# Expert stage of a two-block transformer kernel: the first expert bias added by VectorE instead of TensorE, spread over the partitions by GpSimd

## The reference, cut to what matters

```python
hcat = x_pad[tok] @ w1[e] + b1[e]                 # 128 x 1024 times 1024 x 2048
x_glu = jnp.minimum(hcat[:, ::2], 7.0)
x_lin = jnp.clip(hcat[:, 1::2], -7.0, 7.0)
act = x_glu * jax.nn.sigmoid(1.702 * x_glu) * (x_lin + 1.0)
y = act @ w2[e] + b2[e]                           # 128 x 1024 times 1024 x 1024
```

## Time and profile before

| | us |
|---|---|
| median of 3 runs | 3118.15 |
| lowest and highest | 3116.43, 3118.99 |
| the profiled execution | 3108.3 |
| its span, first to last instruction | 3106.5 |
| TensorE busy in the span | 2924.3 (94%) |
| VectorE busy | 2114.3 (68%) |
| ScalarE busy | 1586.4 (51%) |
| GpSimd busy | 280.5 (9%) |

### The profile page before, as it was taken

One profiled execution on the slowest core, in us unless ns is written; L12 is line 12 of the kernel. 1 busy time (PEld: TensorE's weight loads), 2 busy tenths in 40 slices (PEclk: granted clock), 3 DMA queues, 4 the chain that ended last, 5 costly groups with the idle time before them and its releaser, 6 DMA issues. The chain is left out here.

```text
span 3106.5 us, 46231 instructions
## 1 busy us (share of the span) xinstructions
PE 2924.3 (94%) x18534; PEld 2342.4 (75%) x18534; DVE 2114.3 (68%) x2176; ACT 1586.4 (51%) x1765; POOL 280.5 (9%) x225
## 2 busy tenths in 40 slices
PE   5999999789999999999999959899899999899999
PEld 4777777468887888887888847688778877678877
DVE  6578644569999999989999975466464454366642
ACT  3556433347777777777777734222354542333321
POOL 0110100001111111111111000344000000000000
PEclk9999999789999999999999979899899998999999
DMA  6332343269999999999999972000221222323321
GB/s 247 128 106 89 110 134 109 109 253 367 374 375 363 372 378 375 373 369 371 373 371 369 370 277 68 16 4 4 92 67 59 75 70 81 109 82 94 95 82 68
DMA packets 217372, 607.95 MB, mean 196 GB/s; under 512 B 10784, under 2 KB 118304, under 8 KB 183424
## 3 DMA queue, kind: packets, MB, share of 16 engines
q1 hardware_dynamic: 202480, 554.87, 48.3%
q0 software_dynamic: 14592, 50.36, 4.7%
q10 hardware_dynamic: 144, 0.53, 0.0%
HBM read 582.62 MB, written 23.10 MB: 195 GB/s over the span
## 5 line engine op out<-in xcount | busy, mean ns | idle before, releaser
L2491 DVE TENSOR_TENSOR weight_ring_part<-weight_ring,weight_ring_part 128x2048 fp32r<-128x2048 f32 x380 | 852.9, 2286 | 104.3 <-ACT weight_ring_part L2430 103.5
L2430 ACT ACTIVATE weight_ring_part<-weight_ring 128x2048 fp32r<-128x2048 f32 x380 | 713.7, 1915 | 255.7 <-PE ps L193 137.5
L193 PE MATMUL ps<-weight_ring_part 128*128 128x512 f32 x1456 | 576.8, 396 | 0.0
L189 PE MATMUL ps<-weight_ring_part,gathered_hi 128*128 128x512 f32 x1024 | 408.6, 399 | 0.0
L293 DVE TENSOR_TENSOR weight_ring_part<-weight_ring,weight_ring_part 128x2048 fp32r<-128x2048 f32 x111 | 253.2, 2281 | 225.5 <-ACT weight_ring_part L290 223.6
L193 PE MATMUL ps<-weight_ring_part,gathered_hi 128*128 128x512 f32 x1024 | 405.2, 396 | 0.0
L192 PE MATMUL ps<-weight_ring_part,gathered_lo 128*128 128x512 f32 x1024 | 405.1, 396 | 0.0
L189 PE MATMUL ps<-h1T_hi,weight_ring_part 128*128 128x512 f32 x872 | 357.5, 410 | 3.1 <-DVE weight_ring_part L293 1.7
L192 PE MATMUL ps<-h1T_hi,weight_ring_part 128*128 128x512 f32 x872 | 346.0, 397 | 0.0
L193 PEld LDWEIGHTS ps<-weight_ring_part 128*128 128x128 f32 x1456 | 275.3, 189 | 68.9
L290 ACT ACTIVATE weight_ring_part<-weight_ring 128x2048 fp32r<-128x2048 f32 x111 | 211.1, 1902 | 135.8 <-PE ps L193 104.0
(11 more groups left out here) (491 smaller groups left out, 4382.9 us busy)
## 6 DMA issues: line engine op xcount, KB each, us to landing
weight_ring<-in_w SPq DMA_DIRECT2D x190, 2048.0 KB, 8.8
weight_ring<-in_w_in SPq DMA_DIRECT2D x58, 1024.0 KB, 5.2
weight_ring<-in_w_ffn_up SPq DMA_DIRECT2D x44, 512.0 KB, 4.9
weight_ring<-in_w_ffn_down SPq DMA_DIRECT2D x11, 1024.0 KB, 4.8
mod_tile<-in_w_ada POOLq DMA_DIRECT2D x36, 256.0 KB, 3.1
weight_ring<-in_w_ada SPq DMA_DIRECT2D x8, 1024.0 KB, 12.9
gate_rows<-in_w_ada POOLq DMA_DIRECT2D x28, 256.0 KB, 3.1
weight_ring<-in_w_branch SPq DMA_DIRECT2D x6, 1024.0 KB, 5.2
```

Of the source, the lines that this page charges most:

```text
L189: first = nc.tensor.matmul(out, x[0], y[0], start=start, stop=False)
L193: return nc.tensor.matmul(out, x[0], y[1], start=False, stop=stop)
L2430: nc.scalar.activation(hi_half(h), full_half(h), ACT.Copy).then_inc(w_rounded, 1)
L2491: nc.vector.tensor_tensor(lo_half(h), full_half(h), hi_half(h), ALU.subtract).then_inc(w_split, 1)
```

## The change

b1 is loaded as two rows of 1024 numbers, into partition 0 of a tile that is free by then and of a new one. GpSimd spreads each to all 128 partitions (`spread_bias`, two partition broadcasts of 1024 elements). TensorE's four bias matmuls go, and so do the rounding and the split of b1; the first product now opens the PSUM bank. VectorE adds the bias while it reads PSUM: first both pieces of `glu`, then both of `lin`, then, after a drain, one clamp of the whole `lin` (128 x 1024). `glu` is clamped by GpSimd (`clamp`, two pieces of 512), and ScalarE's activation waits for that. On GpSimd's queue the clamp of expert e+1 stands ahead of the scatter of e, and the spread of e+2 behind it. SyncE loads the next b1 once the last one is spread. The scatter gets a bound, so that slots without a token are skipped.

```diff
-        b1_pick = sb(experts, "b1_pick", [36, 4], F32R)
-        b1_full = sb(experts, "b1_full", [4, 512])
-        b1_parts = sb(experts, "b1_parts", [36, 512], F32R)
+        b1_late = sb(experts, "b1_late", [1, DFF])
+        b1_rows = (gate_rows[0:1, 0, :], b1_late[:, :])
+        b1_wide = sb(experts, "b1_wide", [P, 2 * DFF])
...
-                    sp.dma_start(b1_full[:, :], row.rearrange("e (n f) -> (e n) f", n=4)).then_inc(b1_loaded, 16)
+                    for n in range(2):
+                        sp.dma_start(b1_rows[n], row[:, DFF * n:DFF * n + DFF]).then_inc(b1_loaded, 16)
...
                     if t.more:
-                        sp.wait_ge(used, t.half(0)[0] + (1 + free0))
+                        sp.wait_ge(b1_ready, t.i + 1)
                         load_b1(t.e + 1)
...
+                def spread_bias(r, e):
+                    pool.wait_ge(b1_loaded, 32 * (r * E + e) + 32)
+                    if e:
+                        pool.wait_ge(bias_added, r * E + e)
+                    for n in range(2):
+                        last = nc.gpsimd.partition_broadcast(b1_wide[:, DFF * n:DFF * n + DFF], b1_rows[n], channels=P)
+                    last.then_inc(b1_ready, 1)
+
+                def clamp(r, e):
+                    for s in range(2):
+                        half = slice(512 * s, 512 * s + 512)
+                        pool.wait_ge(glu_ready, (r * E + e) * 2 + (s + 1))
+                        nc.gpsimd.tensor_scalar(glu[:, half], glu[:, half], LIMIT, None, ALU.min).then_inc(glu_clamped, 1)
+
                 def scatter(r, e):
                     pool.wait_ge(y_read, r * E + e + 2)
-                    nc.gpsimd.indirect_dma_start(y_rows, bass.IndirectOffsetOnAxis(y_at[:, e:e + 1], 0), y_out[:, e % 2, :], None)\
+                    nc.gpsimd.indirect_dma_start(y_rows, bass.IndirectOffsetOnAxis(y_at[:, e:e + 1], 0), y_out[:, e % 2, :], None,
+                                                 bounds_check=TOPK * T - 1, oob_is_err=False)\
                         .then_inc(y_stored[e % 2], 16)
...
                     for e in range(3):
                         gather(r, e)
+                    spread_bias(r, 0)
+                    clamp(r, 0)
+                    spread_bias(r, 1)
...
                             gather(r, e + 3)
                         if e:
                             freed(e - 1)
+                        if e + 1 < E:
+                            clamp(r, e + 1)
                         scatter(r, e)
+                        if e + 2 < E:
+                            spread_bias(r, e + 2)
...
                 def up(t):
-                    pe.wait_ge(b1_ready, t.i + 1)
                     pe.wait_ge(up_read, t.i + 1)
-                    for n in range(4):
-                        nc.tensor.matmul(ps[:, n, :], b1_pick[:, n:n + 1].to_broadcast([36, P]), b1_parts[:, :], start=True, stop=False)
...
-                            last = product(nc, ps[:, n, :], (x_hi, x_lo), (w_hi[:, f], w_lo[:, f]), False, k == DK - 1)
+                            last = product(nc, ps[:, n, :], (x_hi, x_lo), (w_hi[:, f], w_lo[:, f]), k == 0, k == DK - 1)
...
-                        if t.more:
-                            round_b1(t.i + 1)
                         for s in range(2):
-                            act.wait_ge(glu_ready, t.i * 2 + (s + 1))
+                            act.wait_ge(glu_clamped, t.i * 2 + (s + 1))
...
-                        if t.more:
-                            split_b1(t.i + 1)
-
+                        dve.wait_ge(b1_ready, t.i + 1)
                         dve.wait_ge(used, t.half(7)[0] + (1 + free0))
+                        halves = [slice(512 * s, 512 * s + 512) for s in range(2)]
+                        pairs = [ps[:, 2 * s:2 * s + 2, :].rearrange("p b (n two) -> p b n two", two=2) for s in range(2)]
+                        bias = [b1_wide[:, 1024 * s:1024 * s + 1024].rearrange("p (b n two) -> p b n two", b=2, two=2) for s in range(2)]
                         for s in range(2):
-                            pairs = ps[:, 2 * s:2 * s + 2, :].rearrange("p b (n two) -> p b n two", two=2)
-                            half = slice(512 * s, 512 * s + 512)
-                            nc.vector.tensor_scalar(glu[:, half].rearrange("p (b n) -> p b n", b=2), pairs[:, :, :, 0], LIMIT, None,
-                                                    ALU.min).then_inc(glu_ready, 1)
-                            last = nc.vector.tensor_scalar(lin[:, half].rearrange("p (b n) -> p b n", b=2), pairs[:, :, :, 1], -LIMIT, LIMIT,
-                                                           ALU.max, ALU.min)
-                        last.then_inc(up_read, 1)
+                            nc.vector.tensor_tensor(glu[:, halves[s]].rearrange("p (b n) -> p b n", b=2), pairs[s][:, :, :, 0], bias[s][:, :, :, 0], ALU.add)\
+                                .then_inc(glu_ready, 1)
+                        for s in range(2):
+                            nc.vector.tensor_tensor(lin[:, halves[s]].rearrange("p (b n) -> p b n", b=2), pairs[s][:, :, :, 1], bias[s][:, :, :, 1], ALU.add)
+                        dve.drain().then_inc(up_read, 1)
+                        nc.vector.tensor_scalar(lin[:, :], lin[:, :], -LIMIT, LIMIT, ALU.max, ALU.min).then_inc(bias_added, 1)
```

More of the change, by code:

```diff
@@ L2252, in experts_pass @@
             (hot_ready, table_ready, table_read, x_turned, xg_rounded, xg_ready, up_read,
-             glu_ready, act_ready, hidden_ready, turned, hid_rounded, hid_ready, y_read, y_free,
-             b1_loaded, b1_rounded, b1_ready, w_rounded, w_split, b2_summed, b2_added, used, *loaded) = sems
+             glu_ready, glu_clamped, bias_added, act_ready, hidden_ready, turned, hid_rounded, hid_ready, y_read, y_free,
+             b1_loaded, b1_ready, w_rounded, w_split, b2_summed, b2_added, used, *loaded) = sems
             b2_banks = lambda t: ps[:, (0, 2, 6, 6)[t]:(0, 2, 6, 6)[t] + 2, :]
@@ L2430, in round_half @@
                     nc.scalar.activation(hi_half(h), full_half(h), ACT.Copy).then_inc(w_rounded, 1)
-                def round_b1(n):
-                    act.wait_ge(b1_loaded, n * 16 + 16)
-                    nc.scalar.activation(b1_parts[0:4, :], b1_full[:, :], ACT.Copy).then_inc(b1_rounded, 1)
                 def round_inputs(n):
@@ L2448, in prologue @@
                 def prologue(t):
-                    round_b1(t.i)
                     if rounds:
@@ L2480, in on_scalar @@
                 with when_needed(act):
-                    nc.scalar.activation(b1_pick[:, :], K["b1_pick"][0:36, 0:4], ACT.Copy)
-                    nc.scalar.activation(b1_parts[:, :], const[0:36, 0:512], ACT.Copy, scale=0.0)
-                    act.drain()
                     act.nop().then_inc(y_read, 1)
@@ L2491, in split_half @@
                     nc.vector.tensor_tensor(lo_half(h), full_half(h), hi_half(h), ALU.subtract).then_inc(w_split, 1)
-                def split_b1(n):
-                    dve.wait_ge(b1_rounded, n + 1)
-                    nc.vector.tensor_tensor(b1_parts[32:36, :], b1_full[:, :], b1_parts[0:4, :], ALU.subtract).then_inc(b1_ready, 1)
                 def split_inputs(n):
@@ L2523, in prologue @@
                         dve.drain().then_inc(up_read, 1)
-                    split_b1(t.i)
                     if rounds:
@@ L2582, in build @@
         pass_sems = ["hot_ready", "table_ready", "table_read", "x_turned", "xg_rounded", "xg_ready", "up_read",
-                     "glu_ready", "act_ready", "hidden_ready", "turned", "hid_rounded", "hid_ready", "y_read", "y_free",
-                     "b1_loaded", "b1_rounded", "b1_ready", "w_rounded", "w_split", "b2_summed", "b2_added", "halves_used"]
+                     "glu_ready", "glu_clamped", "bias_added", "act_ready", "hidden_ready", "turned", "hid_rounded", "hid_ready", "y_read", "y_free",
+                     "b1_loaded", "b1_ready", "w_rounded", "w_split", "b2_summed", "b2_added", "halves_used"]
         first_tiles = ring.units[block2_at:block2_at + 2]
```

## The result

| | before | after |
|---|---|---|
| median of 4 runs each, us | 3117.29 (3115.12 to 3118.99) | 3325.31 (3320.13 to 3334.63) |
| ratio, 95% interval | | 1.0675 [1.0659, 1.0691] |
| span of the profiled execution, us | 3106.5 | 3318.3 |
| first product of the last expert, us | 1769.8 | 1978.8 |
| mean turn, experts 4 to 30, us | 36.64 | 44.40 |

The two executions differ by 211.8 us, and 209.0 of them have built up by the first product of the last expert: the whole loss lies in the turns of the expert stage. The forecast was 3171 us, with a range up to 3245. The direction and the mechanism held; the size did not.

The account below looks back on a forecast made before the run. TensorE was taken to bound the expert stage at 36.53 us a turn; GpSimd's new ring of waits, 19.4 + 18.9 = 38.3 us, adds 1.8 us a turn, +53 us over about 30 turns: 3118 + 53 = 3171 us, range 3084 to 3245.

Parts of the forecast that it names:

- the mechanism: Expert stage: GpSimd loads code sets twice per expert inside a ring of waits longer than TensorE's turn; +53 us, chance 0.52.
- What bounds it: Expert stage before the change: TensorE, busy 100 of 100 us, sets each expert's turn of 36.53 us.
- VectorE's sum: VectorE per turn: 3.32 us of new work (four adds, drain, clamp) against 3.12 us removed, so 0.20 us later.
- TensorE's share: TensorE per turn: the four bias matmuls go, minus 1.12 us, leaving a floor of 35.41 us.
- ring of waits: Per expert: clamp, activation, roundings, read-out, scatter, spread, gather, next clamp, each waiting for the one before; 19.4 us without loads.
- The load stands behind the wait: Rival at GpSimd's clamp: code load starts only after VectorE's add, 6.1 us a turn, 3301 us; chance 0.06.
- the port: VectorE and GpSimd sharing SBUF access: broadcasts and splits delay each other; nothing for TensorE, 2 us kept for the range.
- The ring is then 19.4 + 18.9 = 38.3 us: GpSimd's lap per expert: 19.4 us of work plus 18.9 us for two code loads, 1.8 us over TensorE's 36.53.
- The load's price: Each GpSimd code load, sized from weight-tile landings of 9.7 and 9.2 us: 18.9 us the pair (0 to 24.2).
- I cost both at nothing: SyncE's two b1 loads of 4 KB and the DMA share of 0.95: no cost, 0.5 us a turn either way.
- the hidden case: Rival: GpSimd's lap stays under 35.4 us, turn 35.66 us, 26 us gained, 3092 us; chance 0.35.
- No change: Rival: loads of 8.3 to 8.8 us each, so gain and loss meet; chance 0.07.

Follow-up runs that it names:

- one_set_for_both: product_in_place_of_clamp with one GpSimd code set, holding both broadcast and tensor_tensor, loaded once ahead of the first spread: 3107.44 us, 0.9968 of before.
- product_in_place_of_clamp: Changed kernel with GpSimd's clamp of glu replaced by a tensor_tensor multiplying glu by itself, set changes kept: 3302.1 us, 1.0600 of before.
- scatter_bound_alone: Kernel before the change with only the scatter's bound added, so slots without a token are skipped: 3117.62 us, 1.0009 of before.
- opened kernels: Changed-kernel variants, such as glu's clamp left out (3115.65 us) or on VectorE (3120.0 us), or b1 spread only for expert 0 (3104.84 us).
- spread_ahead_of_scatter: Changed kernel with the spread of e+2 moved ahead of the scatter of e on GpSimd's queue: 3188.36 us, 1.0234 of before.

## Why the prediction was wrong

**What bounds it, VectorE's sum, TensorE's share: right.** Four adds at 0.60, one clamp at 0.69, no b1 split. They decided nothing here.

**The mechanism: right.** The set changes twice per expert, each change is a real load, both lie in a ring of waits, and the ring is longer than TensorE's turn. one_set_for_both against product_in_place_of_clamp shows it. "The load stands behind the wait" is refuted, and so is the port as the cause; it is a part of the ring's length.

**The step that failed is the sum "The ring is then 19.4 + 18.9 = 38.3 us".** Every term was too small, in the lap shown above:

| term | forecast | measured |
|---|---|---|
| two clamps, to the second activation | 1.3 | 3.12 (1528.15 to 1531.27) |
| second activation to the gather's end, without the new work | 15.06 | 10.55 + 2.85 + 3.06 = 16.46 |
| two broadcasts | 3.0 | 4.47 |
| two loads | 18.9 | 9.86 + 10.60 = 20.46 |
| ring | 38.3 | 44.51 |

Half a microsecond of the second row is a part that I left out: with the bound the scatter starts 0.84 us after the end of the read-out, and 0.28 before the change. scatter_bound_alone has 0.80 too, without harm, since nothing waits for the scatter there. Most of the rest is the gather, 2.88 for 1.88.

The loads, the one term without a row of its own, were among the best sized: from the first record of the pair to the operation the medians over 32 experts are 7.7 us ahead of the spread and 11.4 ahead of the clamp, 19.1 together. That is partly luck: the rows that stood in for them were landings of weight tiles, 9.7 and 9.2, and neither load's median is near them; the two errors cancel. The clamp was set nearer the memset (0.55 us) and took 1.50, more than the tensor_tensor that was its upper row. Broadcast and gather carry VectorE's splits: a broadcast took 1.30 us alone and 3.29 beside one, and the gather 2.88 where the earlier trace rows have 1.87. In this lap that is 4.47 - 2.60 = 1.9 us and 1.0 us, nearly half of the 6.2 us missing. I had seen that behaviour in the earlier trace rows and kept it for the range.

**What made 16% of the ring a factor of four.** Only the excess over TensorE's turn counts. The forecast ring of 38.3 us was short by 6.2, but the excess was taken as 1.8 us and was 7.8 (44.40 - 36.64); over 30 turns that is 53 against 209 measured.

**The range failed by its own bounds.** The ends given there for clamps, broadcasts and loads (2.8, 5.2, 24.2) make a ring of 15.06 + 32.2 = 47.3 us, or 10.7 x 30 = 323 us. The range stopped at 3245, and the measured case lay between. Bounds that all push a ring the same way have to be carried through to the end. Two smaller slips: loads of 8.8 to 10 us with 2 us of port give 3132 to 3264 us and not 3125 to 3250, and the first split was said to come 0.1 us after TensorE wants it where the sum used 0.25.

**The load's price.** The idle stretch at GpSimd's tensor_tensor in the quiet of the second block is 7.28 us. The Trainium skill, GPSIMD Engine Reference, section "Instruction dispatch", gives about 6 us with no record of its own in the profile. The trace roughly agrees where the DMA engines are idle, at 1.3 us more; beside the weights' traffic the broadcast's load had a median of 7.7 and the clamp's one of 11.4. The rule's figure would have made the ring 31.4 us, hidden, and the sign wrong.

**"I cost both at nothing" (SyncE and DMA), and the hidden case's gain of 0.87 us a turn: wrong.** The opened kernels without loads have turns of 36.2 to 36.8, and the full computation without the gap of the second block gained 7 us of the 26. The landing of one weight tile had 1.1 us of cover, the bias matmuls; when these went, it became the limit. The 35.66 us took the earlier trace rows's DMA share of 0.95 as harmless because the tiles were in time before. The scatter's smaller number of bytes is worth nothing, as forecast.

**No change** was given 0.07 and is what most opened kernels show, but for this other reason.

## What to carry to other kernels

When an engine's instructions need different sets of code, count the changes per loop and see whether anything waits for the work behind them: here such loads cost 14 us at most out of the ring and 195 us in it. Fix it by making the engine's work fit one set or by giving one of the two operations to another engine, and put the next stage's set back where the engine is idle. When a ring is near the bound, size each of its terms at the dearer row, since an error in any one goes to the time in full; and before counting a removed instruction as gain, ask what lands just in time behind it.

## What was not expected of the hardware

- The load of the clamp's set lasts longer than that of the broadcast's: 10.5 to 14.8 us from pair to operation (median 11.4, the 28 clamps that did not wait for the add) against 5.6 to 9.6 (median 7.7). The traces speak for the place: over the 28 clamp loads the DMA engines were busy all the time (mean share 1.00), over the broadcast loads from the third expert on 0.72 to 0.96. Where the share fell, the other load was short too: for expert 30 of product_in_place_of_clamp 6.83 us at a share of 0.68, and at the tensor_tensor of the second block 7.26 us at 0.00. No run moved the loads on purpose to test it. No DMA queue of the page shows either: the instruction queue moved 1.84 MB in the changed kernel and 1.85 before, so where the code comes from is not shown.
- GpSimd's tensor_scalar on 128x512 took 1.48 us at the least, its tensor_tensor on the same tile 1.03. The instruction with fewer inputs is the slower one.
- A MODIFY_POOL_CONFIG record can be as short where a load follows (37 ns in the changed kernel, 11 in spread_ahead_of_scatter) as where none does (8 ns). What tells a real load is the idle time behind the pair.
